# Router logits of a decoder layer in four column strips of TensorE, folded and turned by one product

## The reference

```python
def _block_output(x, attn, pool, w_o, ln2_w, w_rg, b_rg, w_re, b_re, w_gate, w_up, w_down):
    mix = jnp.concatenate([attn..., pool...], axis=-1)
    x = x + mix @ w_o
    return x + _hier_moe(_rms_norm(x, ln2_w), w_rg, b_rg, w_re, b_re, w_gate, w_up, w_down)

def _hier_moe(h, ...):
    lg = (hf @ w_rg).astype(jnp.float32) + b_rg       # 4 group logits
    g_top = jnp.argmax(lg, axis=-1)
    le = (hf @ w_re ...) + b_re                       # 16 expert logits
    # top 1 of 4 groups, top 2 of 4 experts in it, softmax gates
    ...                                               # 16 SwiGLU experts, 2048 x 512 each
```

## Time and profile before

| | |
|---|---|
| median of three runs | 1040.47 us (1038.17 to 1042.26) |
| the profiled execution, span | 1039.9 us |
| PE busy | 943.9 us, 91% |
| PE weight loads busy | 456.8 us, 44% |
| DVE, ACT, POOL busy | 264.6, 135.4 and 46.6 us |
| mean granted clock of PE | 0.971 |
| DMA | 339.19 MB, mean 326 GB/s |
| chain that ended last | PE 72%, DMA 24% |

### The profile page before, as it was taken

How to read it: one execution, slowest core, us unless ns; L and a number is a source line. 1 busy time by engine, 2 the same in 40 slices (tenths; PEclk the granted TensorE clock), 3 DMA queues, 4 the chain that set the end, 5 groups by cost and what they waited for, 6 DMA issues and landing times.

```text
span 1039.9 us, 10198 instructions
## 1 busy us (share of the span) xinstructions
PE 943.9 (91%) x4425; PEld 456.8 (44%) x4425; DVE 264.6 (25%) x377; ACT 135.4 (13%) x301; POOL 46.6 (4%) x85
## 2 busy tenths in 40 slices
PE   6999999999999999999977899996889778997895
PEld 3444434444445666777754334432343223432331
DVE  1105999673143330101133101101011100111001
ACT  4201111121024441000010010001000010100000
POOL 0002100101110000000000000000000000000000
PEclk8999999999999999999987999999999899999998
DMA  9955699954959997419537999999999999999991
GB/s 343 380 187 190 226 404 400 355 189 151 294 225 350 352 363 284 146 45 407 197 135 304 382 373 421 420 422 423 421 420 423 420 422 422 420 422 422 412 396 79
DMA packets 81041, 339.19 MB, mean 326 GB/s; under 512 B 7332, under 2 KB 11278, under 8 KB 56624
## 3 DMA queue, kind: packets, MB, share of 16 engines
q1 hardware_dynamic: 61263, 296.45, 71.8%
q10 hardware_dynamic: 15808, 33.84, 8.7%
q0 software_dynamic: 3920, 8.19, 2.2%
HBM read 329.71 MB, written 12.24 MB: 329 GB/s over the span
## 4 chain that ended last, share of the span: by engine, by line
PE 72%; DMA 24%; DVE 1%; issue 1%; ACT 1%; POOL 0%; SPq 0%; POOLq 0%; DVEq 0%
PE PS L872 70%; DMA ring<-in_w_up 10%; DMA ring<-in_w_gate 4%; DMA ring<-in_w_down 2%; DMA aux<-in_w_up 2%; DMA X<-in_cache_k 2%; DMA aux<-in_w_down 2%; DMA ring<-in_w_in 1%; PE PS L953 1%; DMA x_scr<-Z 1%; DMA X<-x_scr,pidx 1%; PE PS L1153 1%; DVE Z L1763 0%; DVE HT L1763 0%; PE PS L1043 0%
## 5 line engine op out<-in xcount | busy, mean ns | idle before, releaser
L872 PE MATMUL PS<-ring,HT 128*128 128x512 f32 (+2 forms) x1184 | 375.4, 606 | 11.6 <-DMA ring<-in_w_up 6.8
L872 PE MATMUL PS<-ring,Z 128*64 128x512 f32 (+2 forms) x912 | 240.9, 588 | 26.8 <-DMA ring<-in_w_up 7.1
L872 PEld LDWEIGHTS PS<-ring,HT 128*128 128x128 f32 (+2 forms) x1184 | 141.4, 157 | 210.2 <-issue 209.1
L872 PEld LDWEIGHTS PS<-ring,Z 128*64 128x64 f32 (+1 forms) x912 | 84.3, 141 | 150.5 <-issue 145.6
L872 PE MATMUL PS<-HT,ring 128*128 128x288 f32 x512 | 128.4, 409 | 0.6 <-issue 0.6
L872 PEld LDWEIGHTS PS<-HT,ring 128*128 128x128 f32 x512 | 96.0, 190 | 33.4 <-issue 8.2
L872 PE MATMUL PS<-aux,Z 128*64 128x512 f32 (+2 forms) x208 | 72.5, 525 | 3.3 <-DMA ring<-in_w_down 1.7
L872 PE MATMUL PS<-Z,X 128*128 128x256 f32 x128 | 41.2, 455 | 10.7 <-DMA X<-x_scr,pidx 5.0
L872 PEld LDWEIGHTS PS<-Z,X 128*128 128x128 f32 x128 | 32.7, 325 | 27.1 <-issue 13.0
L1823 DVE TENSOR_TENSOR Z<-Z,PS 128x512 f32<-128x512 f32 x8 | 5.5, 687 | 144.5 <-PE PS L872 144.5
L1763 DVE TENSOR_TENSOR Z<-PS,ln2R 128x512 f32<-128x512 f32 x16 | 11.1, 692 | 121.6 <-PE PS L872 121.6
(11 more groups left out here) (208 smaller groups left out, 541.9 us busy)
## 6 DMA issues: line engine op xcount, KB each, us to landing
ring<-in_w_gate SPq DMA_DIRECT2D x27, 2048.0 KB, 21.3
ring<-in_w_up SPq DMA_DIRECT2D x25, 2048.0 KB, 22.0
ring<-in_w_down SPq DMA_DIRECT2D x23, 2048.0 KB, 22.5
ring<-in_w_in ACTq DMA_DIRECT2D x12, 2048.0 KB, 16.5
ring<-in_w_o SPq DMA_DIRECT2D x8, 2048.0 KB, 12.9
ring<-in_cache_v SPq DMA_DIRECT2D x8, 1536.0 KB, 7.6
ring<-in_cache_v SPq DMA_DIRECT2D x32, 384.0 KB, 8.6
aux<-in_w_gate SPq DMA_DIRECT2D x5, 2048.0 KB, 24.7
```

What stands on the lines that cost most here:

```text
L872: return pe.matmul(out, lhsT, rhs, start=start, stop=stop, skip_group_check=True)
```

## The change

The four column blocks c-3 to c are multiplied one behind the other after column c = 3, 7, 11 and 15, each into its own 32 columns of the array and so into its own 32 partitions of bank 5. Each strip accumulates every fourth column. The logits are then in four parts, in partitions 0 to 19, 32 to 51, 64 to 83 and 96 to 115. ACT copies all 128 partitions. In place of the three transposes there are three products whose stationary operand is the 128 x m block of `LG` and whose moving operand is `fold20`, four identities of 20 one above the other: they add the four parts and turn them at once. Since the partitions between the strips are read too, DVE clears bank 5 beforehand; it also makes `fold20`, in the place of norm weights that are no longer needed.

```diff
-    LG = X[0:20, 5728:5728 + TOK]
+    LG = X[:, 5728:5728 + TOK]
+    fold20 = small[:, 32:52]
...
+    router_zero = sem("router_zero")
...
         act.wait_ge(rl_done, 1)
-        act.activation(LG, PS[0:20, 5, 0:TOK], ACT.Copy).then_inc(rl_moved, 1)
+        act.activation(LG, PS[:, 5, 0:TOK], ACT.Copy).then_inc(rl_moved, 1)
...
-        def router_block(c):
-
-            ins = mm(PS[0:20, 5, 0:TOK], wr[:, c, :], x1T[:, c, :], c == 0, c == DC - 1)
+        def router_blocks(c):
+
+            if c % 4 != 3:
+                return
+            if c == 3:
+                pe.wait_ge(router_zero, 1)
+            for j in range(4):
+                ins = mm(PS[32 * j:32 * j + 20, 5, 0:TOK], wr[:, c - 3 + j, :], x1T[:, c - 3 + j, :], c == 3, c == DC - 1)
             if c == DC - 1:
                 ins.then_inc(rl_done, 1)
...
                 if half == 0 and n:
                     turn_column(n - 1)
-                    router_block(n - 1)
+                    router_blocks(n - 1)
             ins.then_inc(wo_done, 1)
         turn_column(DC - 1)
-        router_block(DC - 1)
+        router_blocks(DC - 1)
         pe.wait_ge(rl_moved, 1)
+        pe.wait_ge(router_zero, 2)
         for k, (t0, m) in enumerate(CHUNKS):
-            ins = pe.transpose(PS[0:m, 6, k * 20:(k + 1) * 20], LG[:, t0:t0 + m], eye[0:20, 0:20])
+            ins = mm(PS[0:m, 6, k * 20:(k + 1) * 20], LG[:, t0:t0 + m], fold20, True, True)
         ins.then_inc(lgT_done, 1)
...
+        settle()
+        dve.wait_ge(ot_moved, DEC_B)
+        dve.memset(PS[:, 5, 0:TOK], 0.0).then_inc(router_zero, 1)
+        dve.tensor_reduce(fold20, eye.rearrange("p (j t) -> p t j", t=32)[:, 0:20, :], AX.X, ALU.add).then_inc(router_zero, 1)
         dve.memset(stat[:, 140:155], 1.0).then_inc(root_in, 1)
         did(dve.tensor_tensor(wr, wr, ln2T.unsqueeze(2).to_broadcast([P, DC, 20]), ALU.mult))
```

## The result

| | before | changed |
|---|---|---|
| median | 1038.17 us of 5 (1033.3 to 1042.26) | 1027.73 us of 5; of the four that the ratio uses 1026.95 (1025.71 to 1031.03) |
| ratio | | 0.9899, 95% interval 0.9865 to 0.9933 |
| profiled execution, span | 1039.9 us | 1024.4 us |
| PE busy | 943.9 us | 933.2 us |

One of the five runs of the changed kernel stands apart at 1640.4 us, with a mean clock of 0.559; it is left out of the ratio.

What follows compares the result with a forecast made beforehand. PE was taken to bound the w_o stage, with the expert weight stream following it. A 9.4 us gain there less 0.5 us in the tail gave -8.9 us against 1040.47: 1031.6 us, range 1028.5 to 1036.0.

Steps and rivals of the forecast that it cites:

- What bounds the kernel, and where the gain arises: w_o stage before 536.9 us: each microsecond off PE starts the remaining weight stream, and the end, a microsecond earlier.
- The router block at 0.79 us, 0.30 of it beside the streaming: Each w_o column: router product holds PE 0.79 us, records 0.49, the other 0.30 for switching stationary shape.
- Four strips in the time of one: Router groups in the w_o stage: four strip products take the time of one, 0.81 us a group.
- The prediction's estimate by it: Router groups by the skill's figure: some 0.13 us longer each, gain ahead of the last column 9.0 us, not 9.4.
- The rival with the products one after another: Router groups: four products run serially, 2.24 us a group, gain 5.1, time 1036.6 us; chance 0.05.
- The third transpose: Plain w_o columns: whether its 32 stationary columns need a switch back, costing 2.4 us; taken as none, gain 9.4.
- The rival that had 8.29: Plain w_o columns: the switch stays behind the third transpose, gain 7.0 us, time 1034.0 us; chance 0.14.
- Cover for what is added: VectorE ahead of the w_o stage: at most 0.9 us of added work hidden in 10.99 us idle, price 0.
- The tail: Behind the last column: turning logits by products delays the gather 0.05 to 0.75 us, taken as 0.5.
- Behind the gather: From the gather to the end: a rigid shift, though half-clock stretches may move, about 2 us of time.
- Result: Whole kernel: -9.4 + 0.5 = -8.9 us against the median 1040.47, giving 1031.6 us.

Runs made afterwards that it cites:

- One_strip: Kernel before the change, with router blocks taken four together in the same 20 columns, no strips or clear: 1034.3 us of 12 runs, ratio 0.9961.
- before_b: The kernel before the change run again with no edit, one run: 1038.18 us.
- before_c: The kernel before the change run once more with no edit, one run: 1035.12 us.
- Each_strip: Changed kernel, but each column's router product run at once in strip c mod 4: 1038.84 us of 12 runs, ratio 1.0004 to the kernel before.

## Why the prediction was right or wrong

**What bounds the kernel, and where the gain arises: right.** PE sets the w_o stage and the weight stream follows it. The loads on wo_done 16 stand right behind the last column in both profiles, and D does not get longer when B shrinks: 491.60 to 493.14 in three executions of the changed kernel, 491.97 to 492.77 in three of the one before.

**The router block at 0.79 us, 0.30 of it beside the streaming: right.** One_strip, whose time depends on that split, came out at 136.11 for 136.1. That the 0.30 us come of the change from 128 stationary columns to 20 and back is argued and not shown.

**Four strips in the time of one: right.** The group cost 0.81 us. The Trainium skill's "TensorE: Matmul & The Clock Gate" (Part 3, measured speedup) gives 2.38 times for three strips, and no figure for four. The prediction's estimate by it would have made B 132.2; it was 131.80 or 131.81 in all three executions. The rival with the products one after another is what one_strip runs: 2.25 us a group. That is not what the strips do.

**The third transpose: right.** It needs no switch; plain columns are 8.09. The rival that had 8.29 falls. This transpose has 32 stationary columns and pays nothing, while a router product with 20 pays 0.30 us, so few stationary columns alone do not make the price. What does is open.

**Cover for what is added: right.** 0.59 us in 10.99 of idle.

**The tail: the sign right, the size too large.** I took 0.5 us out of 0.05 to 0.75, on the ground that the clock falls inside the products. It fell behind them, and the three products took 0.79 us. The place of the fall was read from one execution: the clock fell 3.2 us after the last add there, 5.4 us in before_b and 3.6 in before_c. In the three of the changed kernel it fell 4.1 to 4.7 us after it, and the turn was over at 3.7. That the full clock lasted was no part of the reckoning. VectorE slipped by 0.27, and of that 0.06 to 0.2 reached the gather (C 10.41 to 10.55 before, 10.61 to 10.62 after). For B and C together 8.9 us were forecast, and 151.66 - 142.42 = 9.2 measured, taking the mean of three executions.

**Behind the gather: right in kind.** The stretch at half clock after PE's restart was 5.5 us in place of 4, and D still was the same within its spread.

**The time itself: wrong, and the step that failed is the one called Result.** It set the gain against the median of three runs, 1040.47 us. That median was high: of five runs it is 1038.17, of 23 others 1037.9, of 11 more 1038.76. The low end, "1031.6 less 3 for the spread of the runs and the clock", allows for the spread of the runs and not for an error of the reference itself, though three runs 4 us apart leave about 2 us. Of the 3.9 us between 1031.6 and 1027.73 the reference makes 2.3 (1040.47 - 1038.17) and the stages 0.3 (9.2 for 8.9, nearly all of it the tail). The last 1.2 us or so no step accounts for. With every term of the sum exact the forecast would have been 1040.47 - 9.2 = 1031.3, and 3 us less still above the measured time. With 1037.9 and the same 8.9 us it would have been 1029.0, and the range would have held 1027.7. The sum did not use the profiled execution's own length, but that was a warning: its A was the longest of the ten, with three falls of the clock in it, which the granted clock of its early stretches would have told.

**What stays open.** By medians the kernels differ by 10.4 to 11.2 us, by the stages 9.2. The intervals of the ratio (7 to 14 us) hold both. The means of A and D over three executions each are 392.4 and 492.4 before, 390.6 and 492.2 changed. Nothing of the change stands in the parts of A that vary, which come of PE's start, one load and the clock, so the 1.9 us of A are most likely chance; that they are is not shown. Each_strip speaks against a gain from the added instructions, for it has all of them and its ratio is 1.000, but its interval still allows 1.5 us.

## What to carry to other kernels

A small product between full-width ones can cost more than its streaming, here 0.30 us beside 0.49. Collecting four at a time brought 5.1 us (3.6 of it switches, 1.5 work moved behind the stage), and only then running the four side by side another 4.3 us. Read the price from the starts of the neighbours and not from the product's own records, and look for idle time of PE at a dependency as the place for the collected work. When a forecast is made against a few runs, give their median an error of its own, and look at the granted clock and the waits for loads in the early stretches of the profiled execution before its time is taken as typical.

## What was not expected of the hardware

The w_o stage, PE-paced for over 130 us at the full clock, repeats to 0.01 us from one execution to the next, so that 0.1 us can be told in it from a single profiled execution, while whole executions of one kernel lie 8 us apart. In the ten profiled ones most of that is in A: 388.5 to 395.7 us for instructions that are the same but for two of VectorE at its end. The shortest had the shortest wait for the load at about 155 us, 0.53 us, and the longest lost 3.1 us to a stretch at half clock behind 305 us.
